# Row scaling moved to GpSimd, and a new order of VectorE's work at the entries of a two-block network

## Chip, cores and metric

The kernel runs on one core of a Trainium2 chip. The metric is the device time of one execution in microseconds (us), lower is better. Engines are named as in the profile: PE is TensorE, PEld its weight loads, DVE VectorE, ACT ScalarE, POOL GpSimd, SP the engine that issues loads.

## What is computed

256 tokens of 1024 channels pass through two small stacks in fp32. Each sub-layer starts with a norm of the tokens, and adds its product back:

```python
def rms_norm(x, g):
    y = xf * lax.rsqrt(jnp.mean(xf * xf, axis=-1, keepdims=True) + RMS_EPS)
    return (y * g.astype(jnp.float32)).astype(x.dtype)

# first stack: chunk gating mixer, MLP, dilated attention, MLP, then a final norm
h = h + mixer(rms_norm(h, mix_norm_g[layer]))
h = h + jnp.square(jax.nn.relu(rms_norm(h, mlp_norm_g[layer]) @ w_up[layer])) @ w_down[layer]
# second stack: ffn, pool mixer, ffn | ffn, conv mixer, ffn; each norm is modulated, each product gated
h = h + gate * swiglu(modulate(rms_norm(h, norm_g), shift, scale), w_in, w_out)
```

The change touches the line with `rsqrt`: the product of a token row and its inverse root.

## The kernel before

The tokens lie in SBUF as two tiles `t` = 0, 1 of 128 partitions by 1024 channels: `res` is the residual stream, `xn` the scratch tile that takes the normed tokens. Weights come in slabs of 128x2048 through a ring of three. Products are kept exact enough by splitting each operand in a high and a low part: ScalarE writes `w_hi` (L514), VectorE `w_lo` = raw - `w_hi` (L867, the function `ahead`), and TensorE does three matmuls for each product (`up_tile`, `down_tile`, all under L1320).

Each engine has its own program, written out by hand, and they meet at semaphores; an engine runs its program strictly in order. The stacks are joined by entries, one for each norm: gate_in (at the start), mlp0, qkv, mlp1, ffn0, pool, ffn1, ffn2, conv_in, ffn3 and final2. An entry runs as follows:

- TensorE ends the last product, tile 0 first (`acc0_ready`), then tile 1 (`slab_used`), in `acc` (PSUM).
- VectorE adds the product to `res` (`products(t)`, L973; where the product is gated, at pool, ffn1, ffn2, conv_in, ffn3 and final2, it multiplies first, L970) and counts `res_ready[t]` up.
- ScalarE squares the row and sums it (`square`, L536), then splits a weight slab (L514).
- GpSimd makes mean plus epsilon (L478) and raises it to -1/2 (L472): `rstd`, counted in `rstd_ready[t]`.
- VectorE multiplies `res` by `rstd` into `xn` (`scale_tokens`, L882), counted in `xn_ready`.
- TensorE turns the tile, eight 128x128 transposes in two fills of four (`turn_norm`, L1401); ScalarE applies the gain piece by piece from PSUM into `xn` (`norm_out`, L549 or L551); VectorE splits the pieces into `xT_hi` (L888) and `xT_lo` (L889) in `norm_split`, the very first fill in two halves.
- TensorE's `first_chunk` runs tile 0 on the first slab (it waits for the halves by `xT_ready`), turns tile 1, then runs tile 0 on the second slab and tile 1 on both.

VectorE's order inside an entry is `enter`: sums of tile 0, scaling of tile 0, sums of tile 1, both fills of tile 0, scaling of tile 1, a weight split (`before`, none at ffn1), the fills of tile 1, a weight split (`after`). ffn0 stands behind the final norm of the first stack: `last_norm(t)` waits for a root, scales `res` by it and by `gF` (L1144), and its result is squared again. At pool there is no transposing split. At final2 VectorE scales by itself (L1144).

Of the kernel before, what the change touches and what calls it, by code (L numbers as in the profile page):

```python
# [17 lines left out]
ALU = mybir.AluOpType  # L18
# [7 lines left out]
KT = D // P  # L26
TOKENS = 256
TT = TOKENS // P
# [5 lines left out]
FILL = 4  # L34
# [125 lines left out]
def build(nc, x, mix_norm_g, mlp_norm_g, final_norm_g, a_w_in, a_ln_g, a_ln_b, a_w_s, a_b_s, a_w_out,  # L160
# [7 lines left out]
    with ctx:  # L168
        def sb(name, shape, dt=F32):
            return ctx.enter_context(nc.sbuf_tensor(name, shape, dt))  # L170

        def sem(name):
            return ctx.enter_context(nc.semaphore(name))
# [7 lines left out]
        res = sb("res", [P, TT, D])  # L181
        xn = sb("xn", [P, TT, D])
# [14 lines left out]
        rstd = sb("rstd", [P, TT])  # L197
# [61 lines left out]
        res_ready, sumsq_ready, rstd_ready = ([sem(f"{n}{t}") for t in range(TT)]  # L259
                                              for n in ("res_ready", "sumsq_ready", "rstd_ready"))  # L260
        xn_ready = sem("xn_ready")
# [21 lines left out]
        NORM = {n: at[n].norm for n in ("gate_in", "mlp0", "qkv", "mlp1", "final1", "ffn0", "pool", "ffn1", "ffn2",  # L283
                                        "conv_in", "ffn3", "final2")}
        XN = {n: i for i, n in enumerate(n for n in NORM if n != "final1")}

        XT = {n: i for i, n in enumerate(n for n in XN if n not in ("pool", "final2"))}
# [165 lines left out]
        @block.gpsimd  # L453
        def _(pool):
            nc.gpsimd.memset(flip[:, :, :], 0.0).then_inc(consts_ready, 1)
            nc.gpsimd.memset(ones[:, :], 1.0).then_inc(consts_ready, 1)
            nc.gpsimd.memset(neg_half[:, :], -0.5).then_inc(consts_ready, 1)
            pool.wait_ge(consts_ready, 3)
            nc.gpsimd.memset(rel[N_BUCKETS:N_BUCKETS + 1, :], 1.0).then_inc(consts_ready, 1)
            pool.wait_ge(consts_ready, 4)  # L460
            nc.gpsimd.affine_select(out=ident, in_=ident, compare_op=ALU.not_equal, fill=1.0, base=0,
                                    pattern=[[-1, P]], channel_multiplier=1).then_inc(consts_ready, 1)
            nc.gpsimd.affine_select(out=flip[:, 0, :], in_=flip[:, 0, :], compare_op=ALU.not_equal, fill=1.0,
                                    base=1 - P, pattern=[[1, P]], channel_multiplier=1).then_inc(consts_ready, 1)
            pool.wait_ge(ws_landed, 16)

            nc.gpsimd.affine_select(out=ws_raw, in_=ws_raw, compare_op=ALU.is_ge, fill=0.0, base=0,
                                    pattern=[[0, GROUPS], [-1, P]], channel_multiplier=1).then_inc(ws_masked, 1)

            def inverse_root(src, dst, ready):  # L470

                nc.gpsimd.tensor_tensor(dst, src, neg_half[:, 0:1], ALU.pow).then_inc(ready, 1)  # L472

            scaled = [0]

            def root_of(src, scale, t, ready):

                nc.gpsimd.tensor_scalar(msq[:, t:t + 1], src, scale, EPS, ALU.mult, ALU.add).then_inc(msq_ready, 1)  # L478
                scaled[0] += 1
                pool.wait_ge(msq_ready, scaled[0])  # L480
                inverse_root(msq[:, t:t + 1], rstd[:, t:t + 1], ready)

            def norm(n, t):
                pool.wait_ge(sumsq_ready[t], n + 1)
                root_of(sumsq[:, t:t + 1], 1.0 / D, t, rstd_ready[t])

            for t in range(TT):
                norm(0, t)
            for t in range(TT):
                pool.wait_ge(var_ready, t + 1)  # L490
                root_of(mv[:, t, 1:2], 1.0, t, ln_rstd)
            for names in (("mlp0",), ("qkv",), ("mlp1",), ("final1", "ffn0"), ("pool",), ("ffn1",), ("ffn2",),
                          ("conv_in",), ("ffn3",), ("final2",)):
                for t in range(TT):
                    for name in names:
                        norm(NORM[name], t)


        @block.scalar
# [343 lines left out]
        def _(dve):  # L843
# [11 lines left out]
            def split_lo(slot, n):  # L855

                if isinstance(n, int):
                    if n >= N_SLABS:
                        return
                    dve.wait_ge(hi_ready, n + 1)  # L860
                    if n >= RING:
                        dve.wait_ge(slab_used, n - RING + 1)
                else:
                    first, i, per = n
                    dve.wait_ge(hi_ready, i * per + (first + 1))
                    dve.wait_ge(slab_used, i * per + (first - RING + 1))
                nc.vector.tensor_tensor(w_lo[:, slot, :], raw[:, slot, :], w_hi[:, slot, :].bitcast(F32),  # L867
                                        ALU.subtract).then_inc(lo_ready, 1)

            def ahead(g, i=None, per=0):  # L870
                n = g + RING
                split_lo(n % RING, n if i is None else (n, i, per))
# [4 lines left out]
                src = tr_ps[:, tr % 2, 0:lo.shape[1] * P].rearrange("p (f n) -> p f n", n=P)  # L877
                nc.vector.tensor_tensor(lo, src, hi.bitcast(F32), ALU.subtract).then_inc(tr_read, 1)  # L878

            def scale_tokens(n, t):  # L880
                dve.wait_ge(rstd_ready[t], n + 1)
                nc.vector.tensor_scalar(xn[:, t, :], res[:, t, :], rstd[:, t:t + 1], None, ALU.mult)\  # L882
                    .then_inc(xn_ready, 1)

            def split_tiles(t, k0, k1):
                src = xn[:, t, k0 * P:k1 * P].rearrange("p (k n) -> p k n", n=P)
                hi, lo = xT_hi[:, k0:k1, t * P:(t + 1) * P], xT_lo[:, k0:k1, t * P:(t + 1) * P]
                own(nc.vector.tensor_copy(hi, src))  # L888
                nc.vector.tensor_tensor(lo, src, hi.bitcast(F32), ALU.subtract).then_inc(xT_ready, 1)  # L889

            def norm_split(name, t):

                for b in range(KT // FILL):
                    k0, k1 = b * FILL, (b + 1) * FILL
                    if (t, b) == (0, 0):
                        dve.wait_ge(y_half, XT[name] + 1)
                        split_tiles(t, 0, FILL // 2)
                        k0 = FILL // 2
                    dve.wait_ge(tr_read, at[name].tr + (KT // FILL) * t + b + 1)
                    split_tiles(t, k0, k1)  # L900

            def enter(name, products, before=(), after=(), last_norm=None):


                products(0)
                if last_norm is not None:
                    last_norm(0)
                scale_tokens(NORM[name], 0)
                products(1)
                if name in XT:  # L910
                    norm_split(name, 0)
                if last_norm is not None:
                    last_norm(1)
                scale_tokens(NORM[name], 1)
                for g in before:
                    ahead(g)
                if name in XT:
                    norm_split(name, 1)
                for g in after:
                    ahead(g)  # L920
# [59 lines left out]
                dve.wait_ge(tr_ready, n + 1)  # L980
                nc.vector.tensor_copy(dst, tr_ps[:, n % 2, 0:dst.shape[1]]).then_inc(tr_read, 1)
            dve.wait_ge(tr_read, 3)
            for t in range(TT):
                scale_tokens(0, t)
            split_lo(0, 0)
            for t in range(TT):
                norm_split("gate_in", t)
                split_lo(1 + t, 1 + t)
# [43 lines left out]
            for n in range(NORM_FILLS):  # L1032
                t, b = divmod(n, KT // FILL)
# [6 lines left out]
            def mlp(name):  # L1040
# [28 lines left out]
                with dve.Fori(0, MLP_BODIES) as i:  # L1069
                    for b in range(MLP_BODY):  # L1070
                        step(2 + b, g + 6 + 4 * b, i, MLP_BODY)

            enter("mlp0", residual(last("mlp0"), 0), [last("mlp0") - 1], [last("mlp0")])
            mlp("mlp0")

            enter("qkv", residual(last("qkv"), 1), [last("qkv") - 1], [last("qkv")])
            p = at["qkv"]
            tr0 = p.tr + NORM_FILLS
# [56 lines left out]
            for t in range(TT):  # L1135
                tiles = (slice(None), slice(None), slice(t * P, (t + 1) * P))
                lo_part(hT_hi[tiles], hT_lo[tiles], p.tr + t, p.split + t)
            enter("mlp1", residual(last("mlp1"), 2), [last("mlp1") - 1], [last("mlp1")])
            mlp("mlp1")

# [92 lines left out]
            for q in range(POOLS):  # L1233
                dve.wait_ge(tr_read, at["pool"].tr + q + 1)
                k = slice(2 * q, 2 * q + 2)
                for f in range(2):
                    n = 2 * q + f
# [535 lines left out]
```

## Time and profile before

| | before |
|---|---|
| median of 3 runs | 1641.51 us (1639.99 to 1641.93) |
| span of the profiled execution | 1638.8 us |
| around the span (median less span) | 2.7 us |
| PE busy | 1559.3 us, 95% |
| DVE busy | 1052.6 us, 64% |
| ACT busy | 708.3 us, 43% |
| POOL busy | 22.1 us, 1% |
| mean granted TensorE clock | 0.959 of full speed |

The profiled execution has no time of its own beside its span; 2.7 us lie between it and the median of the timed runs. Busy shares are means over stages; matmuls are pipelined, so 95% for PE is not PE at its peak. Times of instructions on POOL are rough. In the rows, "[0.37 <-DVE xn L882]" says that the engine sat idle for 0.37 us before this instruction, until that line of that engine released it.

### The profile page before, as it was taken

What the parts mean: (1) busy time and instruction counts of PE and PEld (TensorE: products, weight loads), DVE (VectorE), ACT (ScalarE), POOL (GpSimd) and SP (SyncE); (2) the same over time, 40 slices, a digit from 0 to 9 for tenths busy, and PEclk for the clock granted to TensorE, in tenths of its full rate; (3) what the DMA queues carried; (4) which work ended last, traced back from release to release, by engine and by line L of the source; (5) the groups of instructions that cost most, each with busy time, mean ns of one, the idle gap of its engine ahead of it and who ended that gap; (6) DMA issues with size and microseconds to landing.
All of it is one profiled execution on the core that took longest, in us unless ns stands there. A gap on an engine that the chain in (4) does not pass through costs nothing.

```text
span 1638.8 us, 20523 instructions
## 1 busy us (share of the span) xinstructions
PE 1559.3 (95%) x7069; PEld 1284.2 (78%) x7069; DVE 1052.6 (64%) x1126; ACT 708.3 (43%) x831; POOL 22.1 (1%) x63
## 2 busy tenths in 40 slices
PE   6899999999999999989999799999999999999997
PEld 4778888788787888768888688887788878778886
DVE  4758677546535867667888678887655465665444
ACT  5345444444324454453444344435343454354342
POOL 1000000000000000000000000000000000000000
PEclk9999999999559999989999899999999999999999
DMA  8438877457303788847899258996555546445552
GB/s 259 173 138 306 293 268 253 158 176 262 105 20 136 275 283 286 287 151 234 308 311 322 81 192 301 311 322 220 165 194 179 187 128 224 144 150 194 180 185 85
DMA packets 201893, 345.84 MB, mean 211 GB/s; under 512 B 9531, under 2 KB 105027, under 8 KB 201836
## 3 DMA queue, kind: packets, MB, share of 16 engines
q1 hardware_dynamic: 161420, 267.22, 48.6%
q10 hardware_dynamic: 40416, 77.86, 13.5%
q8 instruction: 35, 0.57, 0.1%
q14 instruction: 22, 0.18, 0.0%
HBM read 343.96 MB, written 1.09 MB: 211 GB/s over the span
## 4 chain that ended last, share of the span: by engine, by line
PE 84%; DVE 8%; ACT 3%; issue 2%; DMA 2%; POOL 1%; SPq 0%; POOLq 0%; DVEq 0%; ACTq 0%
PE up_ps L1320 50%; PE acc L1320 29%; DVE w_lo L867 3%; PE tr_ps L1401 2%; DMA ada_raw<-in_ada_w 1%; PE tr_ps L1320 1%; DVE ada_acc L935 1%; PE tr_ps L1586 1%; ACT w_hi L514 1%; ACT xn L536 1%; ACT xn L551 1%; DVE res L973 1%; DVE xn L970 1%; POOL rstd L472 1%; PE tr_ps L1500 1%
## 5 line engine op out<-in xcount | busy, mean ns | idle before, releaser
L867 DVE TENSOR_TENSOR w_lo<-raw,w_hi 128x2048 fp32r<-128x2048 f32 x245 | 561.1, 2291 | 303.1 <-ACT w_hi L514 301.8
L514 ACT ACTIVATE w_hi<-raw 128x2048 fp32r<-128x2048 f32 x245 | 469.5, 1916 | 313.3 <-PE up_ps L1320 255.5
L1320 PE MATMUL up_ps<-w_hi,xT_hi 128*128 128x512 f32 x1264 | 505.2, 400 | 22.2 <-DVE xT_lo L889 17.0
L1320 PE MATMUL up_ps<-w_hi,xT_lo 128*128 128x512 f32 x1264 | 497.3, 393 | 0.0
L1320 PE MATMUL up_ps<-w_lo,xT_hi 128*128 128x512 f32 x1264 | 496.8, 393 | 0.0
L1320 PEld LDWEIGHTS up_ps<-w_hi,xT_hi 128*128 128x128 f32 x1264 | 240.3, 190 | 74.9 <-issue 17.6
L1320 PEld LDWEIGHTS up_ps<-w_hi,xT_lo 128*128 128x128 f32 x1264 | 240.0, 190 | 51.4
L1320 PEld LDWEIGHTS up_ps<-w_lo,xT_hi 128*128 128x128 f32 x1264 | 240.5, 190 | 47.8
L935 DVE SCALAR_TENSOR_TENSOR ada_acc<-ada_raw,cond,ada_acc 128x512 f32 (+1 forms) x252 | 189.3, 751 | 15.7 <-DMA ada_raw<-in_ada_w 8.0
L1320 PE MATMUL acc<-w_hi,hT_hi 128*128 128x512 f32 x624 | 193.4, 391 | 4.1 <-DVE hT_lo L878 4.1
L1320 PE MATMUL acc<-w_hi,hT_lo 128*128 128x512 f32 x624 | 192.4, 389 | 0.0
L1320 PE MATMUL acc<-w_lo,hT_hi 128*128 128x512 f32 x624 | 192.2, 389 | 0.0
L1320 PEld LDWEIGHTS acc<-w_hi,hT_hi 128*128 128x128 f32 x624 | 116.2, 188 | 29.3 <-DVE hT_lo L878 3.3
L528 ACT ACTIVATE hT_hi<-tr_ps 128x256 fp32r<-128x256 f32 (+1 forms) x122 | 47.8, 441 | 210.4 <-PE tr_ps L1401 203.6
L1320 PEld LDWEIGHTS acc<-w_hi,hT_lo 128*128 128x128 f32 x624 | 117.1, 188 | 24.5
L1320 PEld LDWEIGHTS acc<-w_lo,hT_hi 128*128 128x128 f32 x624 | 117.1, 188 | 24.5
L878 DVE TENSOR_TENSOR hT_lo<-tr_ps,hT_hi 128x256 fp32r<-128x256 f32 (+1 forms) x122 | 55.4, 494 | 77.2 <-ACT hT_hi L528 76.8
L754 ACT ACTIVATE pre<-up_ps 128x256 f32<-128x256 f32 x88 | 33.9, 385 | 134.4 <-PE up_ps L1320 134.3
L536 ACT ACTIVATE xn<-res 128x1024 f32<-128x1024 f32 x24 | 25.7, 1072 | 76.4 <-DVE res L973 67.6
L1172 DVE TENSOR_TENSOR mid<-pre,up_ps 128x256 f32<-128x256 f32 x88 | 34.9, 416 | 22.8 <-ACT pre L754 22.8
L1401 PEld LDWEIGHTS tr_ps<-flip,mid 128*128 128x128 f32 x304 | 36.6, 140 | 11.2 <-issue 4.2
L1401 PE MATMUL tr_ps<-flip,mid 128*128 128x128 f32 x304 | 43.3, 272 | 1.3 <-DVE mod_sum L946 1.3
(121 smaller groups left out, 855.2 us busy)
## 6 DMA issues: line engine op xcount, KB each, us to landing
raw<-in_ffn_w_in SPq DMA_DIRECT2D x176, 512.0 KB, 4.8
ada_raw<-in_ada_w ACTq DMA_DIRECT2D x72, 1024.0 KB, 7.1
raw<-in_ffn_w_out SPq DMA_DIRECT2D x88, 512.0 KB, 4.4
raw<-in_w_up SPq DMA_DIRECT2D x64, 512.0 KB, 4.6
raw<-in_w_down SPq DMA_DIRECT2D x64, 512.0 KB, 4.8
raw<-in_b_w_qkv SPq DMA_DIRECT2D x36, 512.0 KB, 4.5
raw<-in_conv_w_in SPq DMA_DIRECT2D x24, 512.0 KB, 4.7
raw<-in_a_w_in SPq DMA_DIRECT2D x16, 512.0 KB, 6.3
```

The source lines that it names most:

```text
L472: nc.gpsimd.tensor_tensor(dst, src, neg_half[:, 0:1], ALU.pow).then_inc(ready, 1)
L514: nc.scalar.activation(w_hi[:, slot, :], raw[:, slot, :], ACT.Copy).then_inc(hi_ready, 1)
L528: nc.scalar.activation(dst, src, ACT.Copy).then_inc(tr_hi, 1)
L536: nc.scalar.activation(xn[:, t, :], res[:, t, :], ACT.Square, accum_out=sumsq[:, t:t + 1]).then_inc(sumsq_ready[t], 1)
L551: a = nc.scalar.activation(dst, src, ACT.Identity, bias=bias, scale=scale)
L754: nc.scalar.activation(pre[:, t, 0:HALF], up_ps[:, t, 0:HALF], ACT.Silu).then_inc(silu_done, 1)
L867: nc.vector.tensor_tensor(w_lo[:, slot, :], raw[:, slot, :], w_hi[:, slot, :].bitcast(F32), ALU.subtract).then_inc(lo_ready, 1)
L878: nc.vector.tensor_tensor(lo, src, hi.bitcast(F32), ALU.subtract).then_inc(tr_read, 1)
L935: a = nc.vector.scalar_tensor_tensor(out=dst, in0=src, scalar=cond[:, k:k + 1], in1=dst, op0=ALU.mult, op1=ALU.add)
L1172: nc.vector.tensor_tensor(mid[:, t, 0:HALF], pre[:, t, 0:HALF], up_ps[:, t, HALF:UPN], ALU.mult).then_inc(ffn_mid, 1)
L1320: return nc.tensor.matmul(dst, a, b, start=start, stop=stop, skip_group_check=True)
L1401: last = nc.tensor.transpose(dst[:, q * P:(q + 1) * P], tile, ident)
```

## The change

`scale_tokens` moves from VectorE's program into GpSimd's, right behind the root of the same tile, at every entry but final2 (and the final norm inside ffn0). It becomes a `tensor_scalar` with two operations, times `rstd` and times 1.0. GpSimd waits on `rstd_ready` for its own root. VectorE's `enter` has a new order: sums of tile 0, first fill of tile 0 (with its two halves), sums of tile 1, second fill of tile 0, then the weight split and the fills of tile 1.

```diff
@@ GpSimd
+            def scale_tokens(n, t):
+                pool.wait_ge(rstd_ready[t], n + 1)
+                nc.gpsimd.tensor_scalar(xn[:, t, :], res[:, t, :], rstd[:, t:t + 1], 1.0, ALU.mult, ALU.mult)\
+                    .then_inc(xn_ready, 1)
+
             for t in range(TT):
                 norm(0, t)
+                scale_tokens(0, t)
...
                     for name in names:
                         norm(NORM[name], t)
+                        if name not in ("final1", "final2"):
+                            scale_tokens(NORM[name], t)
@@ VectorE
-            def scale_tokens(n, t):
-                dve.wait_ge(rstd_ready[t], n + 1)
-                nc.vector.tensor_scalar(xn[:, t, :], res[:, t, :], rstd[:, t:t + 1], None, ALU.mult)\
-                    .then_inc(xn_ready, 1)
...
-            def norm_split(name, t):
-                for b in range(KT // FILL):
+            def norm_split(name, t, fills=range(KT // FILL)):
+                for b in fills:
...
                 products(0)
                 if last_norm is not None:
                     last_norm(0)
-                scale_tokens(NORM[name], 0)
+                if name in XT:
+                    norm_split(name, 0, (0,))
                 products(1)
                 if name in XT:
-                    norm_split(name, 0)
+                    norm_split(name, 0, (1,))
                 if last_norm is not None:
                     last_norm(1)
-                scale_tokens(NORM[name], 1)
                 for g in before:
                     ahead(g)
...
             dve.wait_ge(tr_read, 3)
-            for t in range(TT):
-                scale_tokens(0, t)
             split_lo(0, 0)
```

## Rows read from the trace of the kernel before

**Rows 1.** Page, part 4: shares by engine of the chain that ended last.

```profile
PE 84%; DVE 8%; ACT 3%; issue 2%; DMA 2%; POOL 1%; SPq 0%; POOLq 0%; DVEq 0%; ACTq 0%
```

**Rows 2.** Chain of waits, TensorE, whole span: total us, times, longest us.

```profile
PE up_ps L1320 <- DVE xT_lo L889: 17.0, 9, 3.7
```

**Rows 3.** Timeline of entry ffn2: start us, us, engine, line [idle before].

```profile
1129.96 0.19 POOL L478 TENSOR_SCALAR msq<-sumsq 128x1 f32<-128x1 f32 x1 [188.98 <-ACT xn L536]
1130.23 0.55 POOL L472 TENSOR_TENSOR rstd<-msq,neg_half 128x1 f32<-128x1 f32 x1
1130.82 0.75 DVE L882 TENSOR_SCALAR xn<-res,rstd 128x1024 f32<-128x1024 f32 x1 [2.13 <-POOL rstd L472]
1131.49 1.22 DVE L970 SCALAR_TENSOR_TENSOR xn<-acc,region 128x1024 f32<-128x1024 f32 x1
...
1132.38 2.91 ACT L551 ACTIVATE xn<-tr_ps,mod,gain 128x128 f32<-128x128 f32 x8 [0.71 <-PE tr_ps L1401]
1132.74 1.23 DVE L973 TENSOR_TENSOR res<-res,xn 128x1024 f32<-128x1024 f32 x1
1133.88 0.29 DVE L888 CAST xT_hi<-xn 128x256 fp32r<-128x256 f32 x1
...
1135.14 1.10 ACT L536 ACTIVATE xn<-res 128x1024 f32<-128x1024 f32 x1
...
1136.41 0.19 POOL L478 TENSOR_SCALAR msq<-sumsq 128x1 f32<-128x1 f32 x1 [5.63 <-ACT xn L536]
...
1137.94 2.28 DVE L867 TENSOR_TENSOR w_lo<-raw,w_hi 128x2048 fp32r<-128x2048 f32 x1
...
1138.95 1.28 PE L1401 MATMUL tr_ps<-flip,xn 128*128 128x128 f32 x8
...
1140.28 0.50 PE L1320 MATMUL up_ps<-w_hi,xT_hi 128*128 128x512 f32 x1
```

**Rows 4.** Timeline of entry ffn0, first tile.

```profile
704.04 2.91 ACT L551 ACTIVATE xn<-tr_ps,mod,gain 128x128 f32<-128x128 f32 x8 [0.71 <-PE tr_ps L1401]
704.88 0.29 DVE L888 CAST xT_hi<-xn 128x256 fp32r<-128x256 f32 x1 [0.52 <-ACT xn L551]
...
705.91 0.43 DVE L889 TENSOR_TENSOR xT_lo<-xn,xT_hi 128x256 fp32r<-128x256 f32 x1
```

**Rows 5.** Timeline of entry qkv.

```profile
293.29 1.04 PE L1401 MATMUL tr_ps<-flip,xn 128*128 128x128 f32 x8
...
296.13 0.43 DVE L888 CAST xT_hi<-xn 128x512 fp32r<-128x512 f32 x1
...
298.89 1.09 PE L1401 MATMUL tr_ps<-flip,xn 128*128 128x128 f32 x8 [0.37 <-DVE xn L882]
...
301.09 0.50 PE L1320 MATMUL up_ps<-w_hi,xT_hi 128*128 128x512 f32 x1 [1.11 <-DVE w_lo L867]
```

**Rows 6.** Timeline of entry pool, second tile.

```profile
910.02 1.22 DVE L970 SCALAR_TENSOR_TENSOR xn<-acc,region 128x1024 f32<-128x1024 f32 x1
...
915.43 8.27 PE L1320 MATMUL tr_ps<-region,xn 128*128 128x128 f32 x48 [4.05 <-DVE xn L882]
```

**Rows 7.** Group by line, GpSimd: count | busy us, mean ns | idle before.

```profile
L467 POOL TENSOR_SCALAR_AFFINE_SELECT region<-region 128x1024 f32<-128x1024 f32 x1 | 1.1, 1093 | 6.8 <-DMA region<-in_a_w_s 6.8
```

**Rows 8.** Timeline of the start: VectorE and GpSimd at work together.

```profile
11.19 0.75 DVE L882 TENSOR_SCALAR xn<-res,rstd 128x1024 f32<-128x1024 f32 x1 [1.80 <-POOL rstd L472]
11.43 0.92 POOL L472 TENSOR_TENSOR rstd<-msq,neg_half 128x1 f32<-128x1 f32 x1
```

**Rows 9.** Timeline of the end: VectorE reads PSUM beside GpSimd.

```profile
1629.83 1.22 DVE L970 SCALAR_TENSOR_TENSOR xn<-acc,region 128x1024 f32<-128x1024 f32 x1 [1.50 <-PE acc L1320]
1629.88 0.55 POOL L472 TENSOR_TENSOR rstd<-msq,neg_half 128x1 f32<-128x1 f32 x1
```

**Rows 10.** Stretches: us, busy us by engine, granted clock, DMA share, GB/s.

```profile
713.00:724.00 11.00, 10.55 (x37) 8.53 (x38) 7.24 (x8) 7.18 (x12) 0.00 (x0) 0.70 0.35 123
1337.00:1346.00 9.00, 8.78 (x35) 7.05 (x36) 6.65 (x11) 5.49 (x13) 0.74 (x2) 0.81 0.25 68
```

## The prediction

> **What bounds the kernel now.** I read the chain that ended last first. TensorE holds 84% of it [rows 1], so only a stretch in which TensorE waits can be shortened or lengthened. The chain of waits names where: nine waits for the first split half of an entry, 17.0 us together [rows 2]. Then I went through the timeline of each entry, because the change touches nothing else. [rows 3] are the entry of ffn2. The reader is to see two relay races in it. Tile 0: GpSimd's root, VectorE's scaling at 1130.82, TensorE's transposes, ScalarE's pass at 1132.38, VectorE's first split at 1133.88. That split could start 0.84 us after ScalarE's pass did, as [rows 4] show where VectorE was idle (704.04 to 704.88), so at 1133.22, but the second tile's sum held VectorE until 1133.97. Tile 1: that sum ended at 1133.97, ScalarE squared it at 1135.14 (it was busy with tile 0 until then), GpSimd started at 1136.41, TensorE turned tile 1 at 1138.95 and ran its next block at 1140.28. Both races matter: between them TensorE has one block of 12 matmuls.
>
> **First tile, scaling moved.** VectorE's pass takes 0.75 us [rows 3]. GpSimd's pass over 128x1024 isn't in the trace. The nearest row is its select over a tile of that shape and type, 1.09 us [rows 7]; I take 1.10. Bounds: 0.75 below (VectorE's own), 2.2 above (twice the select, since this pass has two operations and a scalar operand). GpSimd waits 0.08 us for its own earlier result (1129.96 plus 0.19 to 1130.23), VectorE waits 0.04 (root over at 1130.78, scaling at 1130.82). So tile 0 leaves 1.18 instead of 0.79 us after the root: 0.39 later. At the three entries without a gate (mlp0, qkv, mlp1) this is hidden: TensorE turned tile 0 at 293.29 with no idle time in front [rows 5], the scaling having ended about 1.1 us earlier in that timeline. The start is hidden too, behind the wait for the first weights.
>
> The Trainium skill (GPSIMD Engine Reference, 3.1) gives a best case of about 1.8 cycles per element at 1.2 GHz, which I estimate at 1.5 us for 1024 elements; no row here shows it, and with it the sum below would be about 7 us larger.
>
> **First split, moved ahead of the second tile's sums.** At ffn2 ScalarE's pass starts at 1132.38 + 0.39 = 1132.77 and the split at 1133.61, not 1133.88: TensorE starts 0.27 us earlier. The other gated entries (ffn1, conv_in, ffn3) repeat it. This gain lies ahead of the wait for tile 1, so it only counts if tile 1 isn't later.
>
> **Second tile's sums, now behind that split.** The two halves take 1.46 us (704.88 to 706.34, [rows 4]), as the second one needs ScalarE's fourth piece. The gated sum is two instructions, 1131.49 to 1133.97, 2.48 us. So it ends at 1133.61 + 1.46 + 2.48 = 1137.55, 3.6 us later than before. ScalarE is free by then and squares at once, 2.4 us later than its 1135.14. From there: 1.27 us to GpSimd's first instruction (1135.14 to 1136.41), 0.82 to the root's end (0.19, 0.08, 0.55), 0.08 and 1.10 for the scaling, 0.06 to TensorE: 3.3 us. Tile 1 is turned at 1140.9, and the block behind it (0.9 us of transposes) starts at 1141.8 against 1140.28: **+1.5**. The same sum gives +1.5 for conv_in and ffn3. ffn1 has no weight split ahead of its second block that hid part of this before: +2.0. At qkv the sum of tile 1 moves from 293.49 to the place of the next split, 296.0, is one instruction of 1.22 us and ends at 297.2; tile 1 is turned at 300.5, and the block starts at 301.4 against 301.09 [rows 5]: **+0.3**, as at mlp0 and mlp1. ffn0 has a norm of its own inside (sum, gF scaling, sum of squares, root): square 1.2 later, scaling 0.4 longer, less 0.2 of a wait for weights: +1.4. pool has no split; its second sum no longer stands behind the scaling, starts 1.28 us earlier than 910.02, and 0.39 goes to the slower scaling: the turn at 915.43 [rows 6] comes 0.9 earlier. Late sum: 3x1.5 + 2.0 + 3x0.3 + 1.4 - 0.9 = **7.9 us**.
>
> **GpSimd held by VectorE.** Nothing holds VectorE back for tile 1's root any more, so its weight split (L867, 2.28 us) follows right behind the remaining half of tile 0: it starts 1.1 us after the second sum, and GpSimd asks for its first small instruction 1.3 us after it. Are the two independent? At the start the root took 0.92 us instead of 0.55 while VectorE's scaling ran; it ended 0.41 us after that scaling [rows 8]. At the end it took 0.55 beside an instruction that reads PSUM and one SBUF tile [rows 9]. The weight split reads two SBUF tiles. Bounds: nothing, or the whole of it. I take the whole, nearer to [rows 8] since both operands lie in SBUF. Then GpSimd can start only 3.4 us after the sum instead of 1.3: +2.1 at six entries (mlp0, qkv, mlp1, ffn2, conv_in, ffn3), +1.0 at ffn0, where the weight split starts nearer to the squares, +1.1 at pool: **14.7 us**.
>
> The Trainium skill (SBUF — State Buffer, Who interferes with whom) says that a VectorE instruction with two SBUF inputs and a GpSimd instruction that reads SBUF exclude each other for the whole instruction. Its wording for copies agrees with the 0.92 us; no row of before shows a two-input instruction against GpSimd.
>
> **TensorE's clock.** Long gaps were followed by half speed. The stretch from 1337 had a mean granted clock of 0.81 in 9 us: 3.4 us at 1.2 GHz, 1.7 us lost; that from 713, after a gap of 2.9 us, 0.70 in 11 us: 3.3 us lost [rows 10]. After the change TensorE waits 2 us (unheld) to over 4 us (held) ahead of tile 1's transposes at the seven entries other than ffn0, which falls to the low level already. I take 1.7 for each: **11.9 us**; bounds 0 and 7x3.3 = 23.
>
> **Nothing else.** No DMA is issued differently; SP waits for tile 1's scaling ahead of two loads of bias at qkv, needed only 100 us later. final2 keeps its own scaling on VectorE.
>
> **Sum.** 7.9 + 14.7 + 11.9 = 34.5 us. The profiled execution spans 1638.8 us; the median of the runs is 1641.5, 2.7 us around it, unchanged. 1641.5 + 34.5 = 1676.
>
> **The rivals.**
> A. Late but not held: GpSimd reads beside the weight split. Gaps stay near 2 us, and the low clock comes at about four entries: 7.9 + 4x1.7 = 14.7 us, 1656. For it: [rows 9]; against it: [rows 8].
> B. The scaling pass on GpSimd is about twice the select, 2.2 us: 1.1 more for tile 1 at eight entries and pool (9.9), 1.1 more for tile 0 at the four gated entries and ffn0 (5.5), 0.4 at three others (1.3): +16.7, so 1693 when held and 1673 when not. Nothing in the trace times such a pass.
> C. Faster: TensorE's first block covers tile 1's lateness. At ffn2 that block ran partly at half speed until 1138.95. Were tile 1 scaled by then, the earlier split would count: 4x0.27 + 0.9 = 2 us, 1639.5. It decides only if the second sum's lateness stays under 0.9 us (1138.95 less the end of VectorE's old scaling, 1136.41 + 0.86 + 0.75 = 1138.02); I compute 2.4 for the squares alone. If tile 1 is on time but the 0.39 stands against the 0.27, it is no change.
>
> **How the numbers follow.** Held as summed: 0.52, with its own range 1667 to 1686 (clock from 1.0 to 3 us per entry). A: 0.25. B: 0.17. C 0.03, no change 0.03. Range 1652 to 1693: from A with a cheap clock to B when held; outside it lie C, no change and the tail of the clock. This measurement can tell about 0.2% (3.3 us) from nothing. Faster 0.03, same 0.03, slower 0.94.
>
> **What would show it.** In the profile after: the scaling rows under GpSimd near 1.1 us; the first split at gated entries some 0.3 us earlier behind the first transposes; the second sum behind it; TensorE's wait for GpSimd's scaling of tile 1, absent or 0.4 before, 2 to 4.5 us at every entry; GpSimd's 0.19 us instruction stretched to about 2.3 where a weight split runs beside it (rival A: stays 0.19); mean granted clock below 0.959. I am wrong if GpSimd's pass is far from 1.1, if the small instruction slips in before the weight split and the root too, or if the clock stays up.

## The result and the profile after

The changed kernel takes 1671.5 us (median of 4 runs, 1668.8 to 1674.2) against 1640.8 us before: ratio 1.0187, 95% interval 1.0172 to 1.0201. It is 30.7 us slower; 34.5 were forecast. The profiled execution spans 1670.0 us, 31.2 more than before, with a mean granted clock of 0.949 instead of 0.959.

The page of the changed kernel, part 4, the shares of the chain that ended last ([rows 1] before):

```profile
PE 83%; DVE 8%; POOL 2%; ACT 2%; DMA 2%; issue 2%; SPq 0%; POOLq 0%; DVEq 0%; ACTq 0%
```

GpSimd has gone from 1% to 2%. The chain of waits of the changed kernel, TensorE's waits (us in total, times, longest) and GpSimd's instructions by line ([rows 2] and [rows 7] before):

```profile
PE tr_ps L1403 <- POOL xn L490: 41.9, 14, 5.2
PE up_ps L1322 <- DVE xT_lo L893: 13.4, 9, 3.8
```

```profile
L490 POOL TENSOR_SCALAR xn<-res,rstd 128x1024 f32<-128x1024 f32 x20 | 22.4, 1120 | 2.1
L478 POOL TENSOR_SCALAR msq<-sumsq 128x1 f32<-128x1 f32 x24 | 17.3, 721 | 1557.8 <-ACT xn L545 1557.6
```

TensorE's wait for the first split has fallen from 17.0 to 13.4 us, as the new order intends. In its place stands a wait of 41.9 us at 14 places for GpSimd's scaling (L490); before, TensorE waited 14.2 us at 9 places for VectorE's (L882). GpSimd's pass takes 1.12 us; 1.10 was taken. The tiny instruction ahead of the root (L478) has a mean of 0.72 us, where one that is not held takes 0.19: some of them are held. The timeline of entry ffn2 shows which ([rows 3] before; all of it stands 17.41 us later):

```profile
1147.65 0.55 POOL L472 TENSOR_TENSOR rstd<-msq,neg_half 128x1 f32<-128x1 f32 x1
1148.30 1.12 POOL L490 TENSOR_SCALAR xn<-res,rstd 128x1024 f32<-128x1024 f32 x1
...
1150.22 2.90 ACT L560 ACTIVATE xn<-tr_ps,mod,gain 128x128 f32<-128x128 f32 x8 [1.13 <-PE tr_ps L1403]
1151.06 0.29 DVE L892 CAST xT_hi<-xn 128x256 fp32r<-128x256 f32 x1 [4.96 <-ACT xn L560]
...
1152.43 1.22 DVE L974 SCALAR_TENSOR_TENSOR xn<-acc,region 128x1024 f32<-128x1024 f32 x1
...
1153.68 1.22 DVE L977 TENSOR_TENSOR res<-res,xn 128x1024 f32<-128x1024 f32 x1
...
1154.94 1.06 ACT L545 ACTIVATE xn<-res 128x1024 f32<-128x1024 f32 x1 [1.82 <-DVE res L977]
...
1155.89 2.28 DVE L876 TENSOR_TENSOR w_lo<-raw,w_hi 128x2048 fp32r<-128x2048 f32 x1
...
1156.17 2.05 POOL L478 TENSOR_SCALAR msq<-sumsq 128x1 f32<-128x1 f32 x1 [6.76 <-ACT xn L545]
...
1158.31 0.55 POOL L472 TENSOR_TENSOR rstd<-msq,neg_half 128x1 f32<-128x1 f32 x1
...
1160.13 1.53 PE L1403 MATMUL tr_ps<-flip,xn 128*128 128x128 f32 x8 [2.75 <-POOL xn L490]
...
1161.32 0.78 PE L1322 MATMUL up_ps<-w_hi,xT_hi 128*128 128x512 f32 x1
```

Taken back by 17.41 us, the first split starts at 1133.65 (1133.61 was forecast, 1133.88 before), the second sum ends at 1137.49 (1137.55), tile 1 is turned at 1142.72 (1143.0 with the hold), and the block behind it starts at 1143.91 against 1140.28. The reader is to see L876 and L478 side by side: the weight split starts at 1155.89 and ends at 1158.17, GpSimd's instruction over one column starts at 1156.17 and ends at 1158.22, 0.05 us behind it. At qkv, without a gate, it is the same ([rows 5] before, 4.23 us later here):

```profile
302.35 2.28 DVE L876 TENSOR_TENSOR w_lo<-raw,w_hi 128x2048 fp32r<-128x2048 f32 x1
...
302.63 2.04 POOL L478 TENSOR_SCALAR msq<-sumsq 128x1 f32<-128x1 f32 x1 [5.82 <-ACT xn L545]
...
306.59 1.34 PE L1403 MATMUL tr_ps<-flip,xn 128*128 128x128 f32 x8 [3.88 <-POOL xn L490]
...
307.57 0.78 PE L1322 MATMUL up_ps<-w_hi,xT_hi 128*128 128x512 f32 x1
```

The turn waits 3.88 us for GpSimd ahead of 306.59 instead of 0.37.

A table of all entries makes the sum. "Block" is how much later than before TensorE starts the block behind tile 1's turn, "entry" how much longer it takes from GpSimd's first instruction of this entry to that of the next one; both are taken from the start times in the two timelines, counted from GpSimd's first instruction of the entry. Pool has no such block: its entry figure stands in parentheses in the first row, and its one turn starts 0.33 us later than before.

| entry | mlp0 | qkv | mlp1 | ffn0 | pool | ffn1 | ffn2 | conv_in | ffn3 | sum |
|---|---|---|---|---|---|---|---|---|---|---|
| block, us | 2.10 | 2.25 | 2.87 | 2.19 | (-0.09) | 2.39 | 3.63 | 3.29 | 4.07 | 22.7 |
| entry, us | 3.75 | 3.39 | 5.93 | 1.56 | -0.09 | 2.39 | 4.89 | 3.74 | 5.14 | 30.7 |
| L478 of tile 1, us | 2.04 | 2.04 | 2.05 | 0.98 | 0.99 | 0.19 | 2.05 | 2.05 | 2.05 | |

The other 0.5 us lie ahead of mlp0. 22.7 us are lost up to that block and 8.0 behind it. The forecast had 7.9 + 14.7 = 22.6 for the late sums and the hold, and 11.9 for the clock; run 5 shows that part of the 22.7 is the clock too.

One more thing is in this trace: the hold works the other way round as well. At pool GpSimd's scaling of tile 0 runs when VectorE reaches the sum of tile 1 (timeline):

```profile
924.53 1.12 POOL L490 TENSOR_SCALAR xn<-res,rstd 128x1024 f32<-128x1024 f32 x1
925.11 1.60 DVE L977 TENSOR_TENSOR res<-res,xn 128x1024 f32<-128x1024 f32 x1
```

The sum, with both inputs in SBUF, takes 1.60 us where it takes 1.22 at ffn2 above: the engine that is second pays.

### The profile page after: what moved, and what is told of

Read it like the earlier page. It is cut to its first block, busy times and chain, and to the rows that moved or that the text cites. A ratio compares the mean times of both kernels' runs of the same rounds, so it can differ in the third digit from the quotient of the medians.

```text
span 1670.0 us, 20523 instructions
## 1 busy us (share of the span) xinstructions
PE 1569.9 (94%) x7069; PEld 1292.0 (77%) x7069; DVE 1037.9 (62%) x1106; ACT 709.0 (42%) x831; POOL 56.8 (3%) x83
## 3 DMA queue, kind: packets, MB, share of 16 engines
HBM read 343.96 MB, written 1.09 MB: 207 GB/s over the span
## 4 chain that ended last, share of the span: by engine, by line
PE 83%; DVE 8%; POOL 2%; ACT 2%; DMA 2%; issue 2%; SPq 0%; POOLq 0%; DVEq 0%; ACTq 0%
PE up_ps L1322 49%; PE acc L1322 28%; PE tr_ps L1403 3%; DVE w_lo L876 2%; DMA ada_raw<-in_ada_w 1%; DVE res L977 1%; DVE ada_acc L939 1%; PE tr_ps L1322 1%; PE tr_ps L1588 1%; POOL msq L478 1%; POOL xn L490 1%; ACT xn L545 1%; ACT w_hi L523 1%; DVE xn L974 1%; POOL rstd L472 1%
## 5 line engine op out<-in xcount | busy, mean ns | idle before, releaser
L876 DVE TENSOR_TENSOR w_lo<-raw,w_hi 128x2048 fp32r<-128x2048 f32 x245 | 561.0, 2291 | 310.6 <-ACT w_hi L523 310.5
L1322 PE MATMUL up_ps<-w_hi,xT_hi 128*128 128x512 f32 x1264 | 510.1, 404 | 14.8 <-DVE xT_lo L893 13.4
L1322 PEld LDWEIGHTS acc<-w_lo,hT_hi 128*128 128x128 f32 x624 | 117.6, 188 | 24.6
L1322 PEld LDWEIGHTS acc<-w_hi,hT_lo 128*128 128x128 f32 x624 | 117.5, 188 | 24.6
L1403 PE MATMUL tr_ps<-flip,xn 128*128 128x128 f32 x160 | 29.3, 343 | 46.1 <-POOL xn L490 41.9
L478 POOL TENSOR_SCALAR msq<-sumsq 128x1 f32<-128x1 f32 x24 | 17.3, 721 | 1557.8 <-ACT xn L545 1557.6
L892 DVE CAST xT_hi<-xn 128x512 fp32r<-128x512 f32 (+1 forms) x45 | 16.7, 371 | 79.2 <-ACT xn L560 49.1
L1403 PEld LDWEIGHTS tr_ps<-flip,xn 128*128 128x128 f32 x160 | 23.4, 175 | 53.5 <-POOL xn L490 48.2
```

The lines of the kernel that those rows point to most:

```text
L1322: return nc.tensor.matmul(dst, a, b, start=start, stop=stop, skip_group_check=True)
L1403: last = nc.tensor.transpose(dst[:, q * P:(q + 1) * P], tile, ident)
```

## The experiments

Each run was timed against the kernel before on the same chip as the run. Runs 1, 2, 3 and 5 share a median of 1640.7 us for it; runs 4, 6, 7 and 9, made on another chip, 1641.5; the two of run 8, 1642.2.

**1. The new order alone.** VectorE scales; only `enter` is changed (and `norm_split` takes its fills as an argument, as in the change).

```diff
                 scale_tokens(NORM[name], 0)
+                if name in XT:
+                    norm_split(name, 0, (0,))
                 products(1)
                 if name in XT:
-                    norm_split(name, 0)
+                    norm_split(name, 0, (1,))
```

> VectorE scales as before; only its order is new (first fill of tile 0, then the sums of tile 1). By my theory lateness of tile 1 alone costs: the second sum ends 3.2 us later at gated entries, scaling then weight split follow in a row, so the block behind starts about 2.1 us later at ffn2, conv_in and ffn3, 1.2 at ffn1, 1.3 at mlp0, qkv and mlp1, 0.8 at ffn0: 12 us, and 2 to 8 more for TensorE's clock: 1654 to 1660. GpSimd's small instruction stays at 0.19 us. Rival, that GpSimd's pass is the whole cost: 1641, no change.

Measured: 1658.5 us, ratio 1.0103 (1.0081 to 1.0124). The block behind tile 1's turn starts later by 1.17, 1.18, 1.16 (mlp0, qkv, mlp1), 1.13 (ffn0), 1.54 (ffn1), 1.93, 1.93, 1.92 (ffn2, conv_in, ffn3): 12.0 us, as worked out. Another 6.5 us are lost behind the blocks, 2.5 of them at ffn3, where the granted clock is 0.50 for 6.8 us from just ahead of the block; 2 to 8 were expected for the clock. GpSimd's instruction, and the wait that now stands first on TensorE, in this run:

```profile
L478 POOL TENSOR_SCALAR msq<-sumsq 128x1 f32<-128x1 f32 x24 | 4.6, 192 | 1578.4 <-ACT xn L536 1578.2
```

```profile
PE tr_ps L1403 <- DVE xn L882: 28.7, 13, 3.6
```

Its mean of 0.19 us says that nothing is held, and still TensorE waits 28.7 us for tile 1 (and at some entries tile 0), against 14.2 before. The order is a cost of its own; the rival that only GpSimd's pass costs is out.

**2. The move alone.** GpSimd scales as in the change, VectorE has its old order. VectorE's edit, shown against the kernel before:

```diff
                 products(0)
                 if last_norm is not None:
                     last_norm(0)
-                scale_tokens(NORM[name], 0)
                 products(1)
                 if name in XT:
                     norm_split(name, 0)
                 if last_norm is not None:
                     last_norm(1)
-                scale_tokens(NORM[name], 1)
                 for g in before:
                     ahead(g)
```

> GpSimd scales, VectorE keeps its old order. The sums of tile 1 are early, but the weight split now follows at once and meets GpSimd's root. Theory: the root (or the small instruction ahead of it) is stretched by about 2 us; the block behind tile 1's turn starts about 1.5 us later at ffn2, conv_in, ffn3, 1.1 at mlp0, qkv, mlp1, 0.4 at ffn1, pool gains 1: 8 us, with the clock 8 to 14: 1649 to 1655. Rival, that the order is the whole cost: 1641 or less. Rival, that GpSimd is never held: 1643.

Measured: 1656.9 us, ratio 1.0090 (1.0069 to 1.0110), just above the range. The second sums are early again, and yet GpSimd is held: L478 of tile 1 takes 2.32 us at the same six entries, the whole of a weight split. This run also shows what it is that holds. Without a wait of its own VectorE runs tile 1's sum beside tile 0's root; at ffn0 that sum reads PSUM (`acc`) and one SBUF tile, at ffn1 two SBUF tiles (timelines):

```profile
711.15 1.22 DVE L975 TENSOR_TENSOR res<-res,acc 128x1024 f32<-128x1024 f32 x1 [0.74 <-PE acc L1320]
...
711.68 0.19 POOL L478 TENSOR_SCALAR msq<-sumsq 128x1 f32<-128x1 f32 x1 [2.66 <-ACT xn L545]
```

```profile
945.20 1.22 DVE L975 TENSOR_TENSOR res<-res,xn 128x1024 f32<-128x1024 f32 x1
945.30 1.18 POOL L478 TENSOR_SCALAR msq<-sumsq 128x1 f32<-128x1 f32 x1 [18.17 <-ACT xn L545]
```

The same operation over the same size leaves GpSimd its 0.19 us when one input comes from PSUM, and holds it to 0.05 us behind its own end when both lie in SBUF. So the hold is not a matter of the weight split alone. The block starts 1.2 us later at mlp0 and qkv, 2.0 at mlp1, 1.6 to 2.3 at ffn2, conv_in and ffn3. The two parts cost 17.8 and 16.2 us one by one, 34.0 in sum, and 30.7 together: nearly additive, so neither carries the change and neither is its cure.

**3. The weight split out of the way.** The changed kernel, with the entry's weight split ahead of the first split of tile 0.

```diff
                 if name in XT:
+                    for g in before:
+                        ahead(g)
                     norm_split(name, 0, (0,))
...
-                for g in before:
-                    ahead(g)
+                if name not in XT:
+                    for g in before:
+                        ahead(g)
```

> The changed kernel with the entry's weight split moved ahead of the first split of tile 0, so that nothing with two SBUF inputs runs beside tile 1's root. Theory: GpSimd's small instruction for tile 1 falls from 2.05 to 0.19 us at six entries and tile 1 is turned 2.1 us earlier there, less 0.4 to 0.7 by which the first split is later: 9 us back plus up to 5 of clock: 1657 to 1663. Rival, that the hold costs nothing: 1675, since only the lateness of the first split remains.

Measured: 1651.4 us, ratio 1.0061 (1.0044 to 1.0078): 20.1 us come back, more than the 9 to 14 expected. The timeline of its entry qkv:

```profile
293.58 2.29 DVE L876 TENSOR_TENSOR w_lo<-raw,w_hi 128x2048 fp32r<-128x2048 f32 x1 [3.52 <-ACT w_hi L523]
...
299.59 0.19 POOL L478 TENSOR_SCALAR msq<-sumsq 128x1 f32<-128x1 f32 x1 [6.21 <-ACT xn L545]
...
301.69 1.09 PE L1406 MATMUL tr_ps<-flip,xn 128*128 128x128 f32 x8 [2.02 <-POOL xn L490]
...
302.54 0.48 PE L1325 MATMUL up_ps<-w_hi,xT_hi 128*128 128x512 f32 x1
```

The weight split now runs at 293.58, and GpSimd's instruction of tile 1 is back at 0.19 us (at pool, which this edit leaves alone, it is still 0.99). Of TensorE's wait ahead of the turn 2.02 us are left of 3.88. The block is 0.6 to 0.7 us late at mlp0, qkv and mlp1 (2.1 to 2.9 in the changed kernel) and 1.8 at ffn2, conv_in and ffn3 (3.3 to 4.1). Behind this shorter gap the turn and the block run at full rate (1.09 us for eight transposes, 0.48 for a first matmul, against 1.34 and 0.78 above): part of the hold's price was a low clock behind it. By the block starts, moving the weight split gives back 10.9 us at those six entries; most of the rest comes back behind the blocks, where 8.0 us were lost and now none is.

**4. The wait made explicit.** The changed kernel, with VectorE waiting for tile 1's scaling before the weight split.

```diff
                 for g in before:
+                    dve.wait_ge(xn_ready, 2 * XN[name] + 2)
                     ahead(g)
```

> The changed kernel, but VectorE waits for tile 1's scaling ahead of the entry's weight split. Theory: the hold is gone (0.19 us), tile 1 is turned 2.1 us earlier, but the weight split (2.28 us) now stands behind the scaling and the block behind the turn waits for it, so only about 0.8 us per entry come back: 1664 to 1668. If the weight split were no bound the time would be 1657.

Measured: 1666.1 us, ratio 1.0147 (1.0129 to 1.0166), inside the range. That is 24.6 us above the kernel before on its chip, against 30.7: some 6 us back. L478 is at 0.19 us everywhere, but the second block of TensorE needs the weight split too, and it now stands behind the scaling: at qkv the block starts 2.33 us behind the turn instead of 0.99. Not to be held is worth little where the holder's result is wanted next.

**5. The clock.** The changed kernel with matmuls that nobody reads in the gap before tile 1's turn. They write `up_ps` of tile 1, which the next real matmul clears.

```diff
+            def filler(g, n):
+                for _ in range(n):
+                    mm(up_ps[:, 1, :], xT_hi[:, 0, 0:P], w_hi[:, g % RING, 0:UPN], start=True, stop=True)
...
                         elif s == 0:
+                            filler(g, FILLERS.get(name, 0))
                             turn_norm(name, 1)
```

> The changed kernel with extra matmuls, whose product nobody reads, between TensorE's first block of an entry and the turn of tile 1: 16 at mlp0, qkv, mlp1, 10 at ffn0 and ffn3, 6 at ffn2 and conv_in, 2 at ffn1. They fit in the gaps, so they cost nothing by themselves at full rate. Theory: with TensorE busy the clock doesn't fall behind the gap, and most of the clock's term, 5 to 9 us, comes back: 1662 to 1667, mean granted clock above 0.949. Rival, that the clock costs nothing on the path: 1671 or more.

Measured: 1663.1 us, ratio 1.0125 (1.0104 to 1.0146), 8.3 us back; the mean granted clock of the profiled execution is 0.956. First the entry of mlp1 in the changed kernel, then in this run (timelines, and under each a stretch of 3 us from the turn, its columns as in [rows 10], the granted clock third from the end):

```profile
525.88 1.97 PE L1403 MATMUL tr_ps<-flip,xn 128*128 128x128 f32 x8 [3.87 <-POOL xn L490]
...
527.50 0.78 PE L1322 MATMUL up_ps<-w_hi,xT_hi 128*128 128x512 f32 x1
...
528.08 0.63 PE L1322 MATMUL up_ps<-w_lo,xT_hi 128*128 128x512 f32 x1
...
528.50 0.63 PE L1322 MATMUL up_ps<-w_hi,xT_lo 128*128 128x512 f32 x1
```

```profile
525.88:528.88 3.00, 3.00 (x11) 2.77 (x12) 0.64 (x2) 1.84 (x8) 0.00 (x0) 0.50 0.70 281
```

```profile
519.06 3.79 PE L1322 MATMUL up_ps<-w_hi,xT_hi 128*128 128x512 f32 x16
...
523.10 1.09 PE L1403 MATMUL tr_ps<-flip,xn 128*128 128x128 f32 x8 [0.25 <-POOL xn L490]
...
523.95 0.47 PE L1322 MATMUL up_ps<-w_hi,xT_hi 128*128 128x512 f32 x1
...
524.26 0.39 PE L1322 MATMUL up_ps<-w_lo,xT_hi 128*128 128x512 f32 x1
...
524.49 0.40 PE L1322 MATMUL up_ps<-w_hi,xT_lo 128*128 128x512 f32 x1
```

```profile
523.10:526.10 3.00, 3.00 (x17) 2.62 (x18) 1.10 (x3) 2.31 (x9) 0.00 (x0) 1.00 0.94 323
```

After a gap of 3.87 us the eight transposes took 1.97 us and the matmuls followed each other at 0.42 to 0.58 us. With the gap filled from 519.06 on, 0.25 us of it is left, and they take 1.09 us and 0.23 to 0.31 us apart. GpSimd is held for 2.05 us in both. In this run 20.9 us are lost up to the blocks instead of 22.7, and 2.8 behind them instead of 8.0. 2.4 of the 2.8 are at mlp1. The clock is up at its block, but it falls once more 175 us later, in the same phase (timeline, and a stretch of 2 us):

```profile
697.63 0.73 PE L1322 MATMUL acc<-w_hi,hT_hi 128*128 128x512 f32 x2 [2.54 <-DVE hT_lo L887]
```

```profile
700.00:702.00 2.00, 2.00 (x6) 1.52 (x6) 0.38 (x1) 0.00 (x0) 0.00 (x0) 0.50 1.04 338
```

There TensorE waits 2.54 us for VectorE (1.67 in the kernel before), and the clock is 0.50 for 3.4 us soon after: 0.9 us of wait and 1.7 of clock, the 2.4 within 0.2. VectorE is late since it waits 2.89 us for a transfer of `ada_raw` just ahead (2.03 before). The changed kernel has the same there (2.31 us, then 3.4 us at 0.50), and so has the kernel before with the weight split in halves (2.27 us, run 8), while the other nine profiles have a gap of 1.3 to 1.9 us and no fall. So this loss isn't the filled gap's, and doesn't need the change either.

**6. The same in the kernel before**, around the turn of tile 0 at ffn0, ffn1, ffn2, conv_in and ffn3:

```diff
+                gap = FILLERS.get(name, (0, 0, 0))
+                if gap[0]:
+                    pe.wait_ge(lo_ready, g + 1)
+                filler(g, gap[0])
                 turn_norm(name, 0)
+                filler(g, gap[1])
```

> The kernel before with extra matmuls, whose product nobody reads, in the gaps around the turn of tile 0: 4 to 6 ahead of it and 4 to 6 behind it at ffn0, ffn1, ffn2, conv_in and ffn3. If the low clock at these entries comes from the gaps and is on the path, up to 1.7 us at each come back: 1633 to 1639. Rival, that fillers at the low rate push the turn back or the clock falls anyway: 1641 to 1645.

Measured: 1640.0 us, ratio 0.9991 (0.9982 to 1.0000), with a mean clock of 0.964: a miss, 1 us above the range. The higher clock is there, the time is not. At ffn0, ffn2 and conv_in the block behind tile 1's turn starts 0.01 to 0.02 us earlier: there it waits for the weight split of VectorE, not for TensorE. At ffn1, where no such split stands ahead, it starts 0.86 us earlier; at ffn3 it starts 0.59 us later, as the extra matmuls ran past the gap: tile 0's turn starts 0.71 us after its scaling instead of 0.06, VectorE then waits 0.54 us for ScalarE's half of the turned tile, and its weight split is 0.59 us late. The profiled execution also lost 2.1 us in the phase of qkv, where there are no extra matmuls. A gain of 1 to 2 us can't be told from such differences between executions.

**7. The weight split in two halves**, with pool's second sum ahead of its first scaling, in the kernel before. TensorE's second block starts behind the first half (`lo_half`) and waits for the second (`lo_ready`) in its middle.

```diff
+                for h, ready in ((0, lo_half), (1, lo_ready)):
+                    c = slice(h * SLAB // 2, (h + 1) * SLAB // 2)
+                    nc.vector.tensor_tensor(w_lo[:, slot, c], raw[:, slot, c], w_hi[:, slot, c].bitcast(F32),
+                                            ALU.subtract).then_inc(ready, 1)
...
+                if name == "pool":
+                    products(1)
+                    scale_tokens(NORM[name], 0)
...
```

> The kernel before with the entry's weight split done in two halves, the first of which lets TensorE's second block start, and with pool's second sum ahead of its first scaling. TensorE's wait for the weight split (1.1 us at mlp0, qkv and mlp1, 0.2 at others) goes, and pool's turn comes up to 1.2 us earlier: 1636 to 1638. Rival, that the wait only moves to the middle of the block: 1639 to 1640.

Measured: 1633.1 us, ratio 0.9948 (0.9930 to 0.9967): more than expected. The profiled execution took 1637.0 us at a mean clock of 0.957, four of the other five 1630.6 to 1634.3 at 0.961 or 0.962, so its profile shows less than the median does. Its timeline of qkv ([rows 5] before):

```profile
298.84 2.35 DVE L882 TENSOR_TENSOR w_lo<-raw,w_hi 128x1024 fp32r<-128x1024 f32 x2
...
298.97 1.09 PE L1423 MATMUL tr_ps<-flip,xn 128*128 128x128 f32 x8 [0.37 <-DVE xn L893]
...
300.11 0.50 PE L1338 MATMUL up_ps<-w_hi,xT_hi 128*128 128x512 f32 x1
```

The block now follows the turn at 1.14 us; before it came after 2.20. The halves cost 2.35 us together instead of 2.29.

**8. Each of the two by itself.**

> The kernel before with only the entry's weight split done in two halves. By the profile of the run with halves it starts TensorE's second block 1.1 us earlier at mlp0, qkv and mlp1, 0.6 at ffn0 and 0.2 to 0.3 at conv_in and ffn3, 4 to 5 us: 1636 to 1638. If the 8 us of the run with halves and the exchange at pool were mostly the halves: 1634.

Measured: 1638.1 us, ratio 0.9972 (0.9961 to 0.9983), 4.1 us, the upper end of the range.

> The kernel before with one exchange, at pool alone: VectorE does the sums of tile 1 before the scaling of tile 0. The sums can start 1.28 us earlier, as product and PSUM are ready, and TensorE waits there for the second tile only. In the run with halves the entry of pool was 1.8 us shorter in the profile, 0.5 more than I can account for. Theory: 1.2 to 1.8 us, near the limit of the measurement: 1639 to 1641.

Measured: 1640.0 us, ratio 0.9987 (0.9978 to 0.9996), 2.2 us; pool's turn starts 1.28 us earlier, as worked out. Together 6.3 us by themselves, 8.4 when made together; the intervals are wide enough for these to be one number.

**9. Halves and fillers together** (edits of 6 and 7).

> Both of the runs with halves and with extra matmuls in the kernel before. The gains are in different places and add: 1630 to 1636; if the extra matmuls gain nothing, as the halves alone.

Measured: 1631.8 us, ratio 0.9941 (0.9926 to 0.9955). It beats both kernels. Over the halves alone the matmuls add 1.3 us, less than the spread of the runs. In the profiles they show where the block no longer waits for weights: it starts 1.07 us earlier than before at ffn2 and conv_in, against 0.73 later and 0.30 earlier in the profiled execution of run 7.

## Why the prediction was right

1671.5 us lies in the range and 4.5 us below the predicted 1676; rival A would have been 1656, B 1693.

- **What bounds it**: right. Of the 31.2 us, 22.7 lie between an entry's first root and the block behind tile 1's turn, and TensorE's waits for the scaled tiles carry them (41.9 us for 14.2).
- **First tile, scaling moved**: right. 1.12 us against 1.10 taken, from a select of the same shape. Rival B is out. Where tile 0 can be seen by itself, at the gated entries, its turn starts 0.43 us later for 0.39. From the Trainium skill's best case of 1.8 cycles per element (GPSIMD Engine Reference, 3.1) I had estimated 1.5 us; this pass took 1.12, the measurement decides.
- **First split ahead**: right in place and size (0.23 us earlier at ffn2 for 0.27) and worth nothing, since tile 1 is what the next block waits for.
- **Late second sums**: right. Forecast +1.5 for a gated entry and +0.3 for a plain one without the hold, 7.9 in all. Taking from the blocks what the hold added to L478 (1.86 us at six entries, 0.8 at ffn0 and pool, 12.7 together) leaves 10.0 in the changed kernel and 8.2 in run 5, where the gaps are filled: the 8.2 are the lateness, 1.8 the clock. In run 5 the plain entries have +0.25 each, the gated ones with a weight split +1.4 to +2.0, ffn1 +2.4 and ffn0 +0.7 (+1.4 was forecast). At pool the sum left out that GpSimd's scaling holds VectorE: without tile 1's hold its turn comes 0.46 us earlier (run 4), not 0.9. Run 1 shows lateness alone, with nothing held.
- **GpSimd held**: right in mechanism, and somewhat too large: 12.7 us on L478 for 14.7. The prediction chose the whole hold between two bounds with no row of two SBUF inputs to go by. Runs 2, 3 and 4 show it from three sides: it comes without the new order, goes when the weight split is elsewhere, and goes when VectorE waits; and in run 2 a sum holds GpSimd with two SBUF inputs and doesn't with one. The Trainium skill's rule for two SBUF inputs (SBUF — State Buffer, Who interferes with whom) agrees with all of them: the held instruction ended 0.05 us after the weight split. Rival A is out.
- **TensorE's clock**: right in kind, too large by about as much as the hold. 11.9 us were taken, 1.7 at each of seven entries; 1.8 ahead of the blocks and 8.0 behind them are 9.8. Filling the gaps gives back 1.8 and 5.2 (run 5). The error was to charge every entry alike: ffn1 lost nothing behind its block (entry and block both 2.39), as TensorE waits there 0.85 us ahead of the turn and not at least 2; mlp0 lost 1.65, qkv 1.14, ffn2 1.26, ffn3 1.07. mlp1 lost 3.06, with a second fall far behind its block (run 5). conv_in's 0.45 is small only because the kernel before has a stretch of 3.4 us at 0.50 of its own in that phase, at 1412.5; the eight profiles that keep full rate behind this block are 1.1 to 1.2 us shorter there. The length of the gap alone doesn't say what it costs: in run 2 a gap of 2.92 us at mlp0 was followed by full rate and one of 2.91 us at mlp1 by half rate.
- **Rival C**: out. Tile 1's lateness at ffn2 was 2.4 us at the squares, as computed; 0.9 was the limit.

So the three terms measured 8.2, 12.7 and 9.8 us for 7.9, 14.7 and 11.9, and 0.5 lies ahead of the first entry; the hit doesn't rest on errors that cancel.

What is not settled: why the transfer of `ada_raw` at the end of mlp1's phase comes later in some executions than in others, and what decides behind which of two like gaps the clock falls. The split into terms comes from one profiled execution of each kernel.

## What to carry to other kernels

Before moving work to GpSimd, list what VectorE will run at that time: here an instruction with two SBUF inputs stopped even a one-column instruction of GpSimd until it ended, and taking the wait off VectorE is what let it start first. If it can't be avoided, put the holder where GpSimd has nothing on the path (run 3, 20.1 us back); making it wait gives little when its result is wanted next (run 4, 6 us). In a two-tile relay look at the tile that arrives last: making the first one's split earlier is worth nothing when the second one's sum is what pays for it. And an instruction whose result is waited for can be cut in two: starting the matmuls behind half a weight split gave 4.1 us, and the halves took 0.06 us more than the whole.

## What the runs showed of the hardware

- A VectorE subtraction of two SBUF tiles (2.28 us) held a GpSimd instruction of one column for its whole rest: 2.05 us where the subtraction began 0.28 us earlier, 2.32 where the two began together, 0.98 and 0.99 at ffn0 and pool, where it began 1.35 us earlier, against 0.19 when free. VectorE's own instruction kept its 2.28 us.
- A VectorE sum of two SBUF tiles (1.22 us) held the same instruction for 1.18 us; the sum of an SBUF tile and PSUM left it its 0.19 us (run 2).
- The other way round, GpSimd's scaling of 1.12 us, begun 0.59 us earlier, made that sum of two SBUF tiles take 1.60 us; begun 0.83 us earlier, it made a weight split take 2.43 (run 3, ffn2).
- GpSimd's `tensor_scalar` with two operations over 128x1024 fp32 took 1.12 us, VectorE's with one operation 0.75.
- Behind a gap of 3.87 us at mlp1 TensorE's granted clock was 0.50 (1.2 GHz); with the gap filled by matmuls whose product nobody reads it stayed at 1.00 (2.4 GHz). Such matmuls were worth 8.3 us in the changed kernel, but 1.6 us or nothing in the kernel before, with a like rise of the mean clock (0.007 and 0.005): a higher granted clock is not yet time.
